# The last queries' rotation in three parts, and the sample queries' table zeroed by DMA

## What is computed

```python
q = rope((h @ w_q).reshape(n, t, N_BRANCH, HEADS_PER_BRANCH, HEAD_DIM), pos)
for g, (win, dil) in enumerate(BRANCHES):
    if kv_past is None:
        o, l = dilated_prompt(q[:, :, g], kv_branches[g], win, dil)
    else:
        o, l = dilated_sample(q[:, :, g], kv_branches[g], kv_past[g], win, dil)
wts = jax.nn.softmax(jnp.stack(lses, axis=0), axis=0)
o = jnp.einsum('gnth,gnthe->nthe', wts, jnp.stack(outs, axis=0))
```

## Time and profile before

| | us |
|---|---|
| median of 3 runs | 2862.43 |
| lowest and highest | 2861.31, 2862.93 |
| the profiled execution | 2860.89 |
| its span, first to last instruction | 2859.1 |
| TensorE busy | 2698.0 (94%) |
| VectorE busy | 1367.1 (48%) |
| ScalarE busy | 833.4 (29%) |
| GpSimd busy | 269.3 (9%) |

### The profile page before, as it was taken

How to read it: one execution, slowest core, us unless ns; L and a number is a source line. 1 busy time by engine, 2 the same in 40 slices (tenths; PEclk the granted TensorE clock), 3 DMA queues, 4 the chain that set the end, 5 groups by cost and what they waited for, 6 DMA issues and landing times. The chain is left out here.

```text
span 2859.1 us, 44529 instructions
## 1 busy us (share of the span) xinstructions
PE 2698.0 (94%) x18682; PEld 2564.0 (90%) x18682; DVE 1367.1 (48%) x2273; ACT 833.4 (29%) x1682; POOL 269.3 (9%) x435
## 2 busy tenths in 40 slices
PE   5589999999999999999999999887999999999998
PEld 4478999999999999988888888655999999999998
DVE  7972135423333334756666766655264333333325
ACT  7221122111111112345454454543041111111112
POOL 2300000000000000012232434310000000000000
PEclk7689999999999999999999999988999999999999
DMA  3411111111111111323335546556111111111101
GB/s 96 79 37 50 53 40 49 36 50 49 44 44 44 44 44 45 100 69 79 80 87 134 125 105 144 186 196 228 45 45 45 45 44 44 44 44 44 44 30 61
DMA packets 174495, 205.28 MB, mean 72 GB/s; under 512 B 47334, under 2 KB 129686, under 8 KB 174088
## 3 DMA queue, kind: packets, MB, share of 16 engines
q1 hardware_dynamic: 154512, 159.29, 18.5%
q0 software_dynamic: 19840, 44.00, 6.0%
HBM read 156.73 MB, written 27.82 MB: 65 GB/s over the span
## 5 line engine op out<-in xcount | busy, mean ns | idle before, releaser
L217 PE MATMUL PS<-XH,WH 128*128 128x352 f32 x1920 | 617.8, 322 | 3.7 <-PEq L103 3.7
L218 PE MATMUL PS<-XL,WH 128*128 128x352 f32 x1920 | 619.0, 323 | 0.0
L396 PE MATMUL PS<-HIDH,WH 128*128 128x352 f32 x1536 | 494.9, 323 | 8.1 <-DVE HIDL L331 8.1
L397 PE MATMUL PS<-HIDL,WH 128*128 128x352 f32 x1536 | 494.5, 323 | 0.0
L221 PE MATMUL PS<-XH,WL 128*128 128x352 f32 x1920 | 414.9, 324 | 0.0
L217 PEld LDWEIGHTS PS<-XH,WH 128*128 128x128 f32 x1920 | 362.4, 189 | 4.2 <-issue 4.1
L218 PEld LDWEIGHTS PS<-XL,WH 128*128 128x128 f32 x1920 | 361.3, 188 | 0.1
L347 DVE TENSOR_TENSOR H<-PS,H 128x1056 f32<-128x1056 f32 x128 | 160.8, 1256 | 391.5 <-PE PS L400 391.1
L400 PE MATMUL PS<-HIDH,WL 128*128 128x352 f32 x1536 | 331.6, 324 | 0.0
L221 PEld LDWEIGHTS PS<-XH,WL 128*128 128x128 f32 x1920 | 329.4, 188 | 0.0
L396 PEld LDWEIGHTS PS<-HIDH,WH 128*128 128x128 f32 x1536 | 289.3, 188 | 12.7 <-DVE HIDL L331 12.7
(11 more groups left out here) (384 smaller groups left out, 3427.0 us busy)
## 6 DMA issues: line engine op xcount, KB each, us to landing
RAW<-w_up SPq DMA_DIRECT2D x32, 1024.0 KB, 5.3
RAW<-w_down SPq DMA_DIRECT2D x32, 1024.0 KB, 4.9
KVR<-cache_kv_w SPq DMA_DIRECT2D x18, 1024.0 KB, 10.1
QB<-QA SPq DMA_DIRECT2D x120, 132.0 KB, 2.5
ARAW<-w_q SPq DMA_DIRECT2D x24, 512.0 KB, 4.7
O_SCRATCH<-OT POOLq DMA_DIRECT2D x96, 128.0 KB, 2.7
OB<-O_SCRATCH POOLq DMA_DIRECT2D x24, 512.0 KB, 6.4
RAW<-w_glu SPq DMA_DIRECT2D x16, 512.0 KB, 4.7
```

Of the source, the lines that this page charges most:

```text
L217: nc.tensor.matmul(out, wh(k), xh[:, k, c], start=(k == 0), stop=False)
L218: nc.tensor.matmul(out, wh(k), xl[:, k, c], start=False, stop=False)
L396: nc.tensor.matmul(out, w, m.hidh[:, k, q], start=(k == 0), stop=False)
L397: nc.tensor.matmul(out, w, m.hidl[:, k, q], start=False, stop=False)
```

## The change

VectorE's last rotation (chunk 35) leaves item 143 of step 83. Its first product is made at the end of step 84, its second at the end of step 85, and its two sums at the end of step 86 (`turn_by`). GpSimd's three memsets become three DMAs on its own queue, each of one row of 2048 zeros (8 KB, a new constant) to 128 partitions: the first in step 85 after the wait for `prj`, the other two in step 87 after the wait for `roped`, which moves there from step 85. VectorE waits for 48 on `qb_zero` in place of 3.

```diff
--- before.py
+++ after.py
@@ -1826,13 +1826,13 @@
         dst, src = self.place(c)
         self.nc.vector.tensor_copy(dst, src).then_inc(self.kept[1], 1)
 
-    def zero_queries(self, b):
-        self.nc.gpsimd.memset(self.s.qbl[:, b], 0.0).then_inc(self.qb_zero, 1)
+    def zero_queries(self, pool, b, zero):
+        pool.dma_start(self.s.qbl[:, b], zero.to_broadcast([128, 2 * NSMP * 32])).then_inc(self.qb_zero, 16)
 
     def put_queries(self, dve, pair, kl, r):
 
         s = self.s
-        dve.wait_ge(self.qb_zero, 3)
+        dve.wait_ge(self.qb_zero, 48)
         h0, q0 = 8 * pair + 4 * kl + r, 4 * pair + 2 * kl
         for b in range(3):
             for hh in range(2):
@@ -1867,7 +1867,7 @@
         return [(u - 24 * g - 24, g) for g in range(3) if 0 <= u - 24 * g - 24 < (31 if g < 2 else 13)]
 
     sig = Signals(m, "at")
-    root, rs_step, rope_made = sig("root"), sig("rs_step"), sig("rope_made")
+    root, rs_step, rope_made, turned_by = sig("root"), sig("rs_step"), sig("rope_made"), sig("turned_by")
     tables_in, spilled = sig("tables_in"), sig("spilled")
     prj, kept, swapped, v_moved, rotated, roped = (sig(n) for n in ("prj", "kept", "swapped", "v_moved", "rotated", "roped"))
     swapped = [swapped, sig("swapped1")]
@@ -1944,9 +1944,11 @@
                 items(items_of(u))
             if u == 85:
                 pool.wait_ge(prj, N_GR * N_IT)
+                keys_s.zero_queries(pool, 0, a["c_zero"])
+            if u == 87:
                 pool.wait_ge(roped, 3 * N_GR)
-            if 85 <= u < 88:
-                keys_s.zero_queries(u - 85)
+                for part in range(1, 3):
+                    keys_s.zero_queries(pool, part, a["c_zero"])
             for x, g in mixing(u):
                 if x == 12:
                     for i in range(RO):
@@ -2059,6 +2061,21 @@
                 nc.vector.tensor_tensor(s.rope[:, x], s.rope[:, x], s.rsv[:], ALU.mult).then_inc(rope_made, 1)
             dve.wait_ge(rope_made, 2)
 
+        def turn_by(c, part):
+
+            qa, qb = s.qa[:, c % 2], s.qb(c)
+            if part == 0:
+                dve.wait_ge(swapped[c % 2], swaps(c))
+                nc.vector.tensor_tensor(qa[:], qa[:], s.rope[:, 0], ALU.mult).then_inc(turned_by, 1)
+            elif part == 1:
+                nc.vector.tensor_tensor(qb[:], qb[:], s.rope[:, 1], ALU.mult).then_inc(rotated, 1)
+            else:
+                dve.wait_ge(turned_by, 1)
+                dve.wait_ge(rotated, c + 1)
+                b = c // 3 % 3
+                nc.vector.tensor_tensor(by_tile(s.qt[:, 1, 1], b, 1), by_tile(qa[:, 0:SEQ], b, 0), by_tile(qb[:, 0:SEQ], b, 0), ALU.add)
+                nc.vector.tensor_tensor(s.qs[:, b, 7], qa[:, SEQ:NT], qb[:, SEQ:NT], ALU.add).then_inc(roped, 1)
+
         def rotate(c):
             n, kind = c // 3, c % 3
             g, b = head_branch(n)
@@ -2106,8 +2123,8 @@
                 rotate(3 * n)
             elif j == 8:
                 rotate(3 * n + 1)
-            elif (j == 1 and n) or i == N_GR * N_IT - 1:
-                rotate(3 * n - 1 if j == 1 else 3 * n + 2)
+            elif j == 1 and n:
+                rotate(3 * n - 1)
 
         def maxima(u):
             g, b, t = group(u)
@@ -2148,6 +2165,8 @@
             keep_p(u)
             for x, g in mixing(u):
                 mix.dve_part(dve, x, g)
+            if 84 <= u < 87:
+                turn_by(3 * N_GR - 1, u - 84)
             if 88 <= u:
                 x = u - 88
                 keys_s.put_queries(dve, x // 4, x // 2 % 2, x % 2)
@@ -2711,6 +2730,7 @@
                 for nl in range(4):
                     sm[g, t, 32 * nl:32 * nl + 32, 384 + 32 * b:416 + 32 * b] = np.where((nn == 4 * g + nl) & seen, 0, NEG)[None, :]
     c["c_smask"] = sm
+    c["c_zero"] = np.zeros((1, 2048), np.float32)
     return c
```

## The result

Timed in turns with the kernel before, the changed kernel takes 2865.24 us (median of 20 runs, 2861.34 to 2869.44) against 2861.28 us: ratio 1.002, 95% interval 1.0014 to 1.0027, 5.7 us by the ratio; the two medians are 4.0 us apart. That is slower, since the interval leaves out 1.000, and its middle lies at the 0.2% that the prediction could not tell from none. The profiled execution takes 2865.53 us (span 2863.7, mean clock 0.967), 4.6 us over that of before.

A forecast was written before the change was run, and what follows sets the result against it. The prediction took the handover from attention to the sample stage as the bound: a 10.7 us gain eaten by the wait for zeros (minus 0.1), plus 1 for the clock, gives +0.9 us, 2863.4 us; own range 2861 to 2867.

The forecast's parts named there:

- What bounds the kernel: End of attention: sample keys and scores follow the last output without slack, so each microsecond there counts fully at the end.
- Rival 3: End of attention is covered by something the chain does not show; gain and wait both vanish, 2862.4 us; chance 0.10.
- The rotation out of step 83 and into 84 to 86: Step 84's transpose starts 3.7 us earlier; the rotation's third part delays step 88's score, costing 1.9 us.
- The memsets' stalls, gone: Two stalls of 1.95 us before TensorE scores disappear, counted within the 10.7 us gain; VectorE's 128x4 operation takes 0.17 us.
- The zeros' issue: On GpSimd's queue, the first zero transfer is issued at 1843.0, the other two at 1848.25 and 1848.8.
- The landing: Last zero in at 1859.5, at 0.28 MB/us on GpSimd's queue; VectorE waits about 11 us before step 88's first put.
- The estimate from the Trainium skill: Fixed 2.0 us plus bytes over 436 GB/s: zeros land at 1855.1, a gain of 4.5 us; not used.
- The step that failed: Step 90's maxima taken as 1860.38 before and 1860.3 after, so the wait eats the 10.7 us gain entirely.
- Rival 1: Repeated zero row is read slowly, 0.154 MB/us, so VectorE's step 88 wait ends at 1868.2; 2872 us; chance 0.25.
- Rival 2: Zeros land at 1856.2, 2.4 us gained net, and last output store takes 2.4 instead of 6.17 us; 2856.2; chance 0.10.
- The clock: TensorE stands some 8 us, 1851 to 1859, and the slower clock behind it costs 1 us more, between 0 and 2.
- Moved queues: SP's masks and four loads start 6 us later, through by 1867; GpSimd's later stores and the new constant cost nothing visible.

The follow-up runs named there:

- late_puts: The changed kernel with VectorE's eight query puts moved from steps 88 to 95 into steps 92 to 95, two each; 0.9990, repeated 0.9984, of the kernel before.
- ob_late_puts: The changed kernel with the two OB loads issued behind the zeros and the query puts moved to steps 92 to 95; 0.9997 of the kernel before.
- sp_holds: The changed kernel with SP's last four 1 MB sample-key loads held until the zeros have landed; 1.0025 of the kernel before.

## Why the prediction was right, and where it was off

The forecast was 2863.4 us against 2862.43, within the 0.2%; measured were 2865.24 us (inside the forecast's own range, 2861 to 2867) and 5.7 us more than before by the ratio, just at the bound. The place and the kind of the loss were right: one wait of VectorE for the zeros takes the gain back. Its size was not, and that the time is in the range is in part luck. The kernel before measured 1.2 us less in the later runs; taken as a difference, the range runs from 1.4 us under to 4.6 over before, and 4.0 by the medians is in it, 5.7 by the ratio is not. Step by step:

- **What bounds the kernel: right.** The steps of attention carry through to the sample stage: maxima of step 90 5.6 us later, first sample score 6.3, the time 5.7; the profiled execution ends 4.6 us later, 7.0 by step 83. Rival 3 (something covers it) falls with that, and by late_puts, where 11.0 us at this place gave 9 and 11 of the time.
- **The rotation out of step 83 and into 84 to 86: right.** Forecast for the transposes were 1833.5, 1836.5, 1839.4, 1843.7 and 1847.1; measured by step 83 1833.54, 1836.55, 1839.28, 1843.57 and 1846.98. Step 88's score waits 1.79 us for the last part (forecast 1.9), and starts at 1842.71 (1843.0).
- **The memsets' stalls, gone: right**, 0.17 us throughout (one of 0.27, one of 0.23, where before has one of 0.22 besides the stalls).
- **The zeros' issue: right.** By step 83 1842.7 and 1848.0 (1843.0 and 1848.25).
- **The landing: mis-sized by 2.1 us.** Forecast 1859.5, measured 1861.6 by step 83. The prediction drained 4.2 MB and three stores at 0.28 MB/us from 1844 on. The rate, read in one microsecond of before, held as a mean: from that moment (1841.62 in this execution) to the put the queue moved 4.90 MB in 17.6 us. That is in part luck, for it ran at 0.09 MB/us at first, beside the key loads (0.27 MB from 1840 to 1843, 24.6%), and at 0.34 later (0.68 MB in 2 us). The volume was short: 4.2 MB and three stores of 128 KB are 4.6 MB, 16.4 us and not the 15.5 that it took, and 4.9 MB went. All queues together, at 0.366 to 0.383 MB/us in six kernels, are steadier to count with than one.
- **The estimate from the Trainium skill** ("DMA: Bandwidth & Descriptors", section "Anatomy of one DMA"; landing 1855.1) was 6.5 us too kind. Beside full engines the last zero was 13.0 us under way.
- **The step that failed: what the landing is compared with.** "Before: 1860.38. So the wait eats the 10.7 us entirely." The maxima at 1860.38 are step 91's. Step 90's are at 1856.52, right behind the put whose end the prediction itself took; the transpose at 1857.75 is likewise step 89's. So the gain ahead of the wait was 6.8 us and not 10.7 (1849.7 for 1856.52), and by the prediction's own landing its sum would have been 3.8 + 1 = 4.8 us, not 0.9. With 2.1 us more of landing it is 6.9; measured 6.3 at the first sample score. The two errors have the same sign, so they did not cancel: the forecast's 0.9 us is a sixth of the 5.7 measured.
- **Rival 1: its reason is refuted**, its condition (the last zero after 1864.3) did not come about, and the kernel is slower all the same, by the wait that it named. Rival 2 needed a landing at 1856.2 and a last output store of 2.4 us; measured were 1861.6 and 6.1.
- **The clock: right.** Forecast 1 us for the longer pause; from the maxima of step 90 to the first sample score 0.7 us more than before, with the granted clock at 0.50 behind the wait (forecast near 0.5). TensorE stood 12.9 us and not some 8; from the prediction's own 1860.3, with 1.14 us for the maxima, it would have been over 10.
- **Moved queues: right as far as the change goes**; the output stores' lateness shows as soon as the wait for zeros is taken off (late_puts 2.4 us, ob_late_puts 4.9). SP's last late load landed at 1873.4 by step 83, not by 1867, still ahead of the last stores.
- **The split between two parts was not priced apart.** Had it been, from the same walk, the prediction could have seen that its first half alone is faster and its second alone slower.

## What to carry to other kernels

When a transfer takes the place of a computation, estimate its landing from all bytes that the queues hold in front of it over the rate of full engines, with something on top (the idle tail was 1.4 us in sp_holds), and look first for the last place where its result can be waited for: here moving the wait by four steps turned 0.2% lost into 0.1% gained without touching a transfer. Compare a new wait with the same step of the same loop in the old trace, counted from a work item that both share; a row one step further on hides just what one step costs. And when one wait is removed, ask what was late behind its cover.

## What the hardware showed unexpectedly

- A load of one 8 KB row to 128 partitions ran as fast as one of 128 different rows (1.0020 for both kernels; 0.79 MB in 2 us at 93% of the engines' time). The slow CB row of 64 partitions was not such a case; why that one is slow was not tried.
- With two queues at work, the queue with larger packets had 80% of the time and four times the bytes, at equal packet counts (93 and 94).
- Two memsets of GpSimd back to back held VectorE's 128x4 operation for 3.88 us where it takes 0.17, and the row of a copy from PSUM behind it shows 3.60 for 0.42; whether the copy was held itself or only stood behind the other the rows don't say.
- Moving the same three transfers from GpSimd's queue to SP's, 5 us earlier, changed the landing by 0.9 us only.
- Two profiled executions of the same changed kernel reach step 83's transposes 4.0 us apart (1827.30 and 1823.26), and end 3.2 us apart (2865.53 and 2862.38), while the distances behind agree within 0.4. So what sets these two apart arises ahead of this stage; where, and whether that holds for the other executions, stays open.
